# High and low halves of the weight sums stored apart, and the store queue reordered, in the second block of a retention and window-attention trunk

## The reference

```python
def retention_layer(h, w_in, w_out):
    proj = h @ w_in
    q, k, v, g = jnp.split(proj, [D_MODEL, 2 * D_MODEL, 2 * D_MODEL + RET_WIDTH], axis=-1)
    ...                                     # rotary on q and k, decay tables
    sc = jnp.einsum('bnhid,bnhjd->bnhij', qc, kc) * decay_in[None, None]
    o_inner = jnp.einsum('bnhij,bnhje->bnhie', sc, vc)
    ...                                     # scan over chunks: o_cross, state R
    o = o_inner + o_cross
    mu = jnp.mean(o, axis=-1, keepdims=True)
    var = jnp.mean(jnp.square(o - mu), axis=-1, keepdims=True)
    o = ((o - mu) * lax.rsqrt(var + EPS))
    y = o * jax.nn.silu(g)
    return y @ w_out
```

## Time and profile before

| what | value |
|---|---|
| time, median of 3 runs (lowest to highest) | 2474.63 us (2473.95 to 2478.36) |
| profiled execution, its own time | 2476.94 us |
| its span | 2475.1 us |
| PE busy in the span | 2404.5 us, 97% |
| DVE, ACT, POOL busy | 60%, 27%, 18% |
| share of PE in the chain that ended last | 86% (DVE 7%, DMA 4%) |
| DMA traffic | 625.84 MB, mean 253 GB/s |
| heads of block 1, from one load of chunk 0 to the next | 113.2, 115.3 and 112.6 us after the first |

### The profile page before, as it was taken

How to read it: one execution, slowest core, us unless ns; L and a number is a source line. 1 busy time by engine, 2 the same in 40 slices (tenths; PEclk the granted TensorE clock), 3 DMA queues, 4 the chain that set the end, 5 groups by cost and what they waited for, 6 DMA issues and landing times.

```text
span 2475.1 us, 28627 instructions
## 1 busy us (share of the span) xinstructions
PE 2404.5 (97%) x11216; PEld 1972.0 (80%) x11216; DVE 1484.6 (60%) x2037; ACT 679.7 (27%) x1470; POOL 451.1 (18%) x327
## 2 busy tenths in 40 slices
PE   7999999999989999989999999999999999999998
PEld 6888888877867787878888888888888887888886
DVE  6555655677556656663758564655567745557374
ACT  2212312235121212122442231223352312213143
POOL 2111111221245646550001000000001100001000
PEclk9999999999999999999999999999999999999999
DMA  8667565645789798985259878776447987787433
GB/s 351 270 226 289 212 254 226 236 175 217 302 304 394 289 388 302 385 314 200 98 214 318 286 245 290 249 256 217 143 163 233 330 263 278 255 274 252 170 102 145
DMA packets 131833, 625.84 MB, mean 253 GB/s; under 512 B 8864, under 2 KB 9632, under 8 KB 109728
## 3 DMA queue, kind: packets, MB, share of 16 engines
q1 hardware_dynamic: 122864, 588.53, 65.7%
q10 hardware_dynamic: 8880, 36.18, 3.9%
HBM read 471.58 MB, written 153.09 MB: 252 GB/s over the span
## 4 chain that ended last, share of the span: by engine, by line
PE 86%; DVE 7%; DMA 4%; issue 1%; ACT 1%; POOL 1%; SPq 0%; DVEq 0%; POOLq 0%; ACTq 0%
PE ps L691 27%; PE ps L693 27%; PE ps L692 27%; DMA whl<-comb_w 2%; PE ps L1201 2%; DMA vg_w<-ff 1%; DVE ff L2262 1%; PE ps L1211 1%; PE ps L1009 1%; DVE fr L1660 1%; ACT ff L1498 1%; PE ps L839 1%; DVE mx L2302 1%; DVE xlo L1660 0%; DVE ff L2332 0%
## 5 line engine op out<-in xcount | busy, mean ns | idle before, releaser
L691 PE MATMUL ps<-whl,xhi 128*128 128x512 f32 (+1 forms) x1088 | 420.3, 386 | 4.4 <-DVE xlo L1660 2.8
L693 PE MATMUL ps<-whl,xlo 128*128 128x512 f32 (+1 forms) x1088 | 414.0, 380 | 0.0
L692 PE MATMUL ps<-whl,xhi 128*128 128x512 f32 (+1 forms) x1088 | 413.3, 380 | 0.0
L691 PE MATMUL ps<-xhi,whl 128*128 128x512 f32 x768 | 304.0, 396 | 17.6 <-DVE xlo L1664 16.2
L693 PE MATMUL ps<-xhi,whl 128*128 128x512 f32 x768 | 300.4, 391 | 0.0
L692 PE MATMUL ps<-xlo,whl 128*128 128x512 f32 x768 | 299.7, 390 | 0.0
L691 PE MATMUL ps<-whl,fr 128*128 128x512 f32 x640 | 257.9, 403 | 9.8 <-DMA whl<-comb_w 5.7
L693 PE MATMUL ps<-whl,fr 128*128 128x512 f32 x640 | 255.3, 399 | 0.0
L692 PE MATMUL ps<-whl,fr 128*128 128x512 f32 x640 | 254.6, 398 | 0.0
L691 PEld LDWEIGHTS ps<-whl,xhi 128*128 128x128 f32 x1088 | 206.8, 190 | 43.8 <-issue 4.3
L693 PEld LDWEIGHTS ps<-whl,xlo 128*128 128x128 f32 x1088 | 206.5, 190 | 39.4
(11 more groups left out here) (215 smaller groups left out, 3843.7 us busy)
## 6 DMA issues: line engine op xcount, KB each, us to landing
whl<-split_w SPq DMA_DIRECT2D x60, 2048.0 KB, 8.3
whl<-split_w SPq DMA_DIRECT2D x118, 1024.0 KB, 7.0
split_w<-whl SPq DMA_DIRECT2D x44, 2048.0 KB, 7.2
whl<-vg_w SPq DMA_DIRECT2D x64, 1024.0 KB, 6.9
raw<-in_stream SPq DMA_DIRECT2D x44, 1024.0 KB, 9.4
vg_w<-ff SPq DMA_DIRECT2D x32, 1024.0 KB, 7.6
whl<-comb_w SPq DMA_DIRECT2D x32, 1024.0 KB, 7.1
raw<-in_stream SPq DMA_DIRECT2D x50, 512.0 KB, 11.6
```

The lines of the kernel that those rows point to most:

```text
L691: pe.matmul(dst, lhs[0], rhs[0], start=start, stop=False)
L692: pe.matmul(dst, lhs[0], rhs[1], start=False, stop=False)
L693: return pe.matmul(dst, lhs[1], rhs[0], start=False, stop=stop)
```

## The change

The semaphore `comb_stored` becomes two, `comb_hi_stored` and `comb_lo_stored`, and the pair of stores two functions. A high half is stored as soon as POOL has made it, a low half when it is made.

```diff
-                def store_piece(j):
-
-                    sp.wait_ge(comb_lo.sem, at(comb_lo, j + 1))
-                    for i in range(2):
-                        ...
-                        sp.dma_start(dst.rearrange("(q p) n -> p q n", p=P),
-                                     stage[:, i, :].rearrange("p (q n) -> p q n", q=4)).then_inc(comb_stored.sem, 16)
+                def store_part(j, i):
+
+                    made, stored = ((comb_hi, comb_hi_stored), (comb_lo, comb_lo_stored))[i]
+                    sp.wait_ge(made.sem, at(made, j + 1))
+                    ...
+                    sp.dma_start(dst.rearrange("(q p) n -> p q n", p=P),
+                                 stage[:, i, :].rearrange("p (q n) -> p q n", q=4)).then_inc(stored.sem, 16)
```

The waits follow. POOL's high half of piece j waits for the store of the previous high half and for the previous low half to be made; whoever writes a low half waits for the store of the previous low half:

```diff
                 if j > 0:
-                    pool.wait_ge(comb_stored.sem, at(comb_stored, 2 * j))
+                    pool.wait_ge(comb_hi_stored.sem, at(comb_hi_stored, j))
+                    pool.wait_ge(comb_lo.sem, at(comb_lo, j))
...
                 if own_lo:
                     pool.wait_ge(comb_hi.sem, at(comb_hi, j + 1))
+                    pool.wait_ge(comb_lo_stored.sem, at(comb_lo_stored, j))
...
                             dve.wait_ge(comb_hi.sem, at(comb_hi, j + 1))
+                            if j > 0:
+                                dve.wait_ge(comb_lo_stored.sem, at(comb_lo_stored, j))
```

The loads of T1 to T4 wait for both semaphores, and so do the three places that waited for all stores of a head. SP's order changes, and on DVE the two parts of piece 2's low half each move one state update ahead:

```diff
+                store_hi(0)
                 load_split(at, 3, split_rows(h, 3), CHUNK)
-                store_piece(0)
+                store_lo(0)
                 load_piece(h, 2)
+                store_hi(1)
                 load_split(at, 4, split_rows(h, 4), CHUNK)
-                store_piece(1)
+                store_lo(1)
                 load_piece(h, 3)
+                store_hi(2)
                 load_split(at, 5, split_rows(h, 5), CHUNK)
-                store_piece(2)
+                store_lo(2)
                 load_piece(h, 4)
-                store_piece(3)
+                store_hi(3)
                 sp.wait_ge(o_mm.sem, at(o_mm, 4))
...
                     if c == 6:
+                        store_lo(3)
                         load_piece(h, 5)
+                        store_hi(4)
...
-                return lambda: store_piece(4), lambda: store_piece(5)
+
+                def close():
+                    store_hi(5)
+                    store_lo(5)
+
+                return lambda: store_lo(4), close
```

More of the change, by code:

```diff
@@ L303, in build @@
         comb_lo = count("comb_lo", head=PIECES, since=1)
-        comb_stored = count("comb_stored", head=2 * PIECES, unit=16, since=1)
+        comb_hi_stored = count("comb_hi_stored", head=PIECES, unit=16, since=1)
+        comb_lo_stored = count("comb_lo_stored", head=PIECES, unit=16, since=1)
         t_loaded = [count(f"comb_loaded{q}", head=1, unit=16, since=1) for q in range(4)]
@@ L448, in load_comb @@
                 def load_comb(dst, q):
-                    sp.wait_ge(comb_stored.sem, at(comb_stored, 4))
+                    sp.wait_ge(comb_hi_stored.sem, at(comb_hi_stored, 2))
+                    sp.wait_ge(comb_lo_stored.sem, at(comb_lo_stored, 2))
                     sp.dma_start(dst.bitcast(F32), comb_rows(h, q)).then_inc(t_loaded[q].sem, 16)
@@ L466, in load_piece, with store_hi, store_lo @@
                         sp.dma_start(raw[j % 2][:, i * HALF:(i + 1) * HALF].rearrange("p (a n) -> p a n", a=2), src).then_inc(comb_raw[j % 2].sem, 16)
-                def store_piece(j):
-                    sp.wait_ge(comb_lo.sem, at(comb_lo, j + 1))
-                    for i in range(2):
-                        if j < 2:
-                            dst = comb_w[4 * h * P:4 * (h + 1) * P, i, j * 512:(j + 1) * 512]
-                        else:
-                            dst = vg_w[4 * h * P:4 * (h + 1) * P, i, (j - 2) * 512:(j - 1) * 512]
-                        sp.dma_start(dst.rearrange("(q p) n -> p q n", p=P),
-                                     stage[:, i, :].rearrange("p (q n) -> p q n", q=4)).then_inc(comb_stored.sem, 16)
+                def store_part(j, i):
+                    made, stored = ((comb_hi, comb_hi_stored), (comb_lo, comb_lo_stored))[i]
+                    sp.wait_ge(made.sem, at(made, j + 1))
+                    if j < 2:
+                        dst = comb_w[4 * h * P:4 * (h + 1) * P, i, j * 512:(j + 1) * 512]
+                    else:
+                        dst = vg_w[4 * h * P:4 * (h + 1) * P, i, (j - 2) * 512:(j - 1) * 512]
+                    sp.dma_start(dst.rearrange("(q p) n -> p q n", p=P),
+                                 stage[:, i, :].rearrange("p (q n) -> p q n", q=4)).then_inc(stored.sem, 16)
+                def store_hi(j):
+                    store_part(j, 0)
+                def store_lo(j):
+                    store_part(j, 1)
                 if h == 0:
@@ L561, in _ @@
             post_loads(1, last_stores)
-            sp.wait_ge(comb_stored.sem, Place("head", 1, HEADS - 1)(comb_stored, 2 * PIECES))
+            sp.wait_ge(comb_hi_stored.sem, Place("head", 1, HEADS - 1)(comb_hi_stored, PIECES))
+            sp.wait_ge(comb_lo_stored.sem, Place("head", 1, HEADS - 1)(comb_lo_stored, PIECES))
             for b in range(FAST, BLOCKS):
@@ L638, in comb_piece @@
                 if j > 0:
-                    pool.wait_ge(comb_stored.sem, at(comb_stored, 2 * j))
+                    pool.wait_ge(comb_hi_stored.sem, at(comb_hi_stored, j))
+                    pool.wait_ge(comb_lo.sem, at(comb_lo, j))
                 elif at.h > 0:
-                    pool.wait_ge(comb_stored.sem, Place("head", at.b, at.h - 1)(comb_stored, 2 * PIECES))
+                    pool.wait_ge(comb_hi_stored.sem, Place("head", at.b, at.h - 1)(comb_hi_stored, PIECES))
+                    pool.wait_ge(comb_lo_stored.sem, Place("head", at.b, at.h - 1)(comb_lo_stored, PIECES))
                 pool.tensor_scalar(stage[:, 0, :].bitcast(F32R), raw[j % 2], 1.0, 1.0, ALU.mult, ALU.mult).then_inc(comb_hi.sem, 1)
@@ L2043, in one_head @@
                     state_update(0)
+                    if combine:
+                        comb_less_hi(2, (0,))
                     state_lo(1)
@@ L2047, in one_head @@
                     if combine:
-                        comb_less_hi(2, (0,))
+                        comb_less_hi(2, (1,))
                     state_lo(2)
@@ L2051, in one_head @@
                     state_update(2, 2 if last else 1)
-                    if combine:
-                        comb_less_hi(2, (1,))
                     state_lo(3)
@@ L2218, in one_block @@
                 if combine:
-                    dve.wait_ge(comb_stored.sem, Place("head", b, HEADS - 1)(comb_stored, 2 * PIECES))
+                    dve.wait_ge(comb_hi_stored.sem, Place("head", b, HEADS - 1)(comb_hi_stored, PIECES))
+                    dve.wait_ge(comb_lo_stored.sem, Place("head", b, HEADS - 1)(comb_lo_stored, PIECES))
                 spread(rstd, rdiag_done)
```

## The result

| what | before | after |
|---|---|---|
| median of 4 runs each (lowest to highest) | 2476.29 us (2473.95 to 2478.36) | 2460.36 us (2460.11 to 2462.85) |
| ratio after to before, 95% interval | | 0.9938 [0.9921, 0.9955] |
| profiled execution: own time, span | 2476.94, 2475.1 us | 2460.11, 2458.3 us |

The change makes the kernel 16 us faster, where 27 were forecast: the direction is right, the size is not, and 2460.36 lies 0.4 us outside the range.

A forecast was written before the change was run, and what follows sets the result against it. PE, busy 97% of the span, bounds the kernel. Gains of 33.3 us less 3 + 4.3 for S1 give 26.0; with one more, 27 us, so 2447.6 us; range 2439 to 2460.

The forecast's parts named there:

- T2's wait and its tail: PE's wait for the T2 load in block 1's four heads, 5.7 us, and 1.4 us of slow matmuls, both to go.
- the first gap: PE idle before each head's first transposes (L839), 17.8 us, to go entirely, with its 6.8 us tail of slow matmuls.
- DVE's parts of piece 2: Half of piece 2's low half moved ahead of state_lo(1) on DVE, into idle time; price zero.
- rival (b): Slower: DVE's new wait for piece 1's low half, ahead of state_lo(1), delays cross(1); 2476 to 2482 us; chance 0.06.
- rival (c): Stall at L839 stays, its y tile held by the wait for piece 3's low half; 2472 to 2478 us; chance 0.06.
- the price of POOL's wait for the low store: POOL's low half of piece 4 waits for piece 3's low store, delaying S1: 1 us in three heads, 4.3 in the first.
- queue sum: SP's transfers added at 2.7 us per MB (392 GB/s); second head's low store of piece 3 issued 840.6, landed 848.3.
- 5.4 us for the residual stream: First head: two more MB share SP's queue, 5.4 us, about 4.3 of it reaching S1.
- store takes 11 us: Upper end of the S1 loss allowed in each of three heads: 3 us, against the 1 us taken.
- the 4.4 us: Landing time of a 1 MB store by the skill's price; by that alone POOL's new wait costs nothing, 7 us better.
- rival (a): The gap moves down to S1 and T2 in block 1; 13.5 us of gain remain, 2461 us; chance 0.19.
- gaps of 2 us or more ahead of S1 in all heads: Listed sign that the forecast is wrong: PE idle 2 us or more before S1 in every head of block 1.

The follow-up runs named there:

- Experiment 4: Kernel before, with POOL's power (inverse deviation) moved ahead of the high half of piece 3 in block 1; 2469.18 us, ratio 0.9973.
- experiment 3: Changed kernel with POOL's own low half of piece 4 behind the low y sums, and own low halves cut into four instructions; 2437.00 us, ratio 0.9844.
- Experiments 6: Changed kernel with DVE's two parts of piece 2's low half back in their old places; 2472.68 us, ratio 0.9988.
- 9: Kernel of experiment 3 with DVE's two parts of piece 2's low half back in their old places; 2448.35 us, ratio 0.9883.
- experiment 7: Changed kernel with the load of piece 5 issued behind the high store of piece 4, not ahead of it; 2463.59 us, ratio 0.9956.
- experiment 2: Changed kernel with POOL's own low halves cut into four instructions, in their old place; 2460.44 us, ratio 0.9938.
- Experiment 1: Changed kernel with POOL's own low half of piece 4 moved behind the four low parts of the y sums; 2443.62 us, ratio 0.9878.
- experiments 5: Changed kernel with SP's old order, stores back in pairs, split semaphores kept; 2458.61 us, ratio 0.9932.
- 8: Kernel of experiment 3 with SP's old order, stores back in pairs, split semaphores kept; 2460.04 us, ratio 0.9930.

## Why the prediction was wrong, step by step

| term | forecast, us | read from the rows, us |
|---|---|---|
| idle at the first transposes, slow matmuls behind, the transposes | 26.2 | 26.2 |
| T2's wait and its tail | 7.1 | 7.1 |
| idle at S1 and at the last transposes | -6.3 | -10.8 |
| slow matmuls behind S1 | 0 | -4.6 |
| the end of the block | 0 | -4.3 |
| sum | 27.0 | 13.6 |

The span fell by 2475.1 - 2458.3 = 16.8 us, so 3.2 us of gain stand in no row that I can name. PE's idle time fell by 10.2 us (70.6 to 60.4), of which the rows explain 9.8; the open part lies almost all in the time in which PE is at work. The right column is a reading and not a closed account.

**Right: the first gap.** No head has an idle time before its first transposes. On POOL the high half of piece 3 is done well before the variances, and the power starts 0.1 us behind them (timelines of DVE and POOL, second head; the earlier trace rows have 4.7 us between the two):

```profile
825.65 0.23 DVE L2088 TENSOR_SCALAR ov<-mv,rcol 128x4 f32<-128x4 f32 x1 [0.15 <-DVE mv L2065]
```
```profile
825.97 1.02 POOL L631 TENSOR_TENSOR ors<-ov,mhalf 128x4 f32<-128x4 f32 x1 [6.97 <-DVE ov L2088]
```

Experiment 4 confirms the cause by itself, as far as it goes (three heads of four).

**Right: T2.** Nothing is left of the 5.7 us of the earlier trace rows. A late S1 also gives T2 more time; in experiment 3, where S1 is not late, 2.6 us of the wait come back, in the first head alone.

**Right that it costs nothing, but its worth was not priced: DVE's parts of piece 2.** PE waited nowhere for DVE's new wait, which came to 1.43 us in the first head and to nothing in the others. In the second head the part ends at 808.47 and the low part of the state follows at 808.74, after 0.27 us of waiting for ACT (timeline of DVE, second head):

```profile
807.25 1.22 DVE L1987 TENSOR_TENSOR ff<-raw,ff 128x1024 fp32r<-128x1024 f32 x1
808.74 1.28 DVE L1686 SCALAR_TENSOR_TENSOR fr<-state,rcol,fr 128x1024 fp32r<-128x1024 f32 x1 [0.27 <-ACT fr L1502]
```

That answers rival (b), and with the first gap rival (c) falls too. But "price zero" names only the cost. Experiments 6 and 9 show what the move is good for, 12 and 11 us: it keeps POOL's early high half off the low part of the state, and it sends the low store of piece 2 off 8 us sooner. The second of these was in the forecast's working without a price: the low half made at 823.7 is the second part in its new place; in its old one it would end at 828.33 + 1.22 = 829.55.

**Wrong: the price of POOL's wait for the low store.** This is the step that failed: "I allow 1 us loss in each of three heads", plus 4.3 in the first. The forecast put S1 4.9 us after the end of the gate tiles. PE frees chunk 5 at the end of those tiles, and SP then issues T2, at 841.26; S1 starts at 848.79, 7.5 us later, 2.6 more than forecast. The store accounts for that. By the forecast's queue sum (issued at 840.6, landed at 848.3) it was to take 7.7 us, and it took 10.5 (10.3 to 10.5 in three heads; 13.9 in the first, where the forecast's 5.4 us for the residual stream make 13.1). SP's timeline, second head:

```profile
823.98 0.81 SPq L453 DMA_DIRECT2D fr<-comb_w  x2
829.44 0.53 SPq L453 DMA_DIRECT2D whl<-comb_w  x1
830.02 0.61 SPq L522 DMA_DIRECT2D whl<-split_w  x1
831.81 0.38 SPq L478 DMA_DIRECT2D vg_w<-ff  x1
```

Ahead of it stand 4 MB issued within 8 us, and the DMA engines are full, but at 359 GB/s, not at the 392 of the earlier trace rows that I had used:

```profile
824.00:842.00 18.00, 18.00 (x87) 14.90 (x86) 10.35 (x13) 6.74 (x11) 10.53 (x6) 1.00 1.00 359
```

By the queue sum of the forecast, 5 MB from 824.0 end at 837.5 at 2.7 us each and at 838.6 at 2.92 each, with 2.1 us more at 840.7: that explains 8.9 of the 10.5 us. The last 1.6 us stay open; experiment 7 refutes one cause, what is issued behind. So of the 2.8 us too few 1.1 are the rate and the rest is open. That the median of all stores in the earlier trace rows is 7.7 as well is an accident, and I took it for support, although the same change had put this store behind 4 MB of loads. Over block 1 the stores of the changed kernel land at

```profile
DMA to landing us min/median/max: 5.1/10.5/15.1
```

against 4.2/7.7/15.9 in the earlier trace rows. The 3 us for "store takes 11 us" that the forecast named as its worst case was nearly the ordinary case, and I had taken 1. By the 4.4 us that the forecast worked out from the Trainium skill (SBUF — State Buffer, the DMA setup-cost knee) no wait would have come; no store of block 1 landed that soon in the changed kernel, and it is no price for a store behind a full queue.

**Left out: the slow matmuls.** Each of these waits, 2.8 to 6.5 us, has a tail, as the forecast itself had said of the first gap. At S1 it put the tail at nothing, without a reason. I count about 32 matmuls at 0.43 us behind S1 in four heads against 9 before, 23 x 0.20 = 4.6 us.

**Left out: the port.** I weighed the rule of the Trainium skill on GpSimd and VectorE at one short DVE part, where it came to nothing. It bore on two other places, both beside the own low half, the longest of POOL's instructions in the block. One is the last gate product, 4.95 and 4.73 us in place of 0.69 in the third and fourth head. The forecast had booked 1 us of gain here, on the guess that the two would no longer run side by side. In the first two heads the product starts ahead of POOL and is not held. In the other two DVE took PE's wait over from POOL; experiment 2 shows that it added nothing to it. The other is the end of the block, where the kernel makes rounded copies for the next step. DVE's timelines of the changed kernel and of the kernel before:

```profile
1088.15 3.69 DVE L2229 CAST vwin<-vwin 64x256 fp32r<-64x256 f32 x1
```
```profile
1109.59 0.29 DVE L2205 CAST vwin<-vwin 64x256 fp32r<-64x256 f32 x1
```

POOL's subtraction ran from 1087.14 for 4.55 us, so the copy ended 0.15 us behind it. The rule as cited is on operations with two inputs, and the copy has one; that it was held by the same port is my reading. PE waited 3.75 us for what DVE makes next, 0.82 before, with about 15 half-width matmuls at the lower clock behind it: 2.9 + 1.4 = 4.3 us. In experiment 2, with the four short instructions, this wait is 1.6. In experiments 1 and 3 it is 1.0 and 0.4, but there the copy runs ahead of that subtraction.

**The rivals.** The time is that of rival (a), 2461, but only half of its mechanism came true, and the match of the number is luck. Its 13.5 us do not follow from its terms: less 9 for S1, three tails of 2.2 and the 7.1 of T2, 27 leaves 4.3 us, 2470. S1 is late as it said, with the slow matmuls behind; T2 is not late, and what (a) had for T2 was taken by the end of the block. I had given (a) 0.19 and cut the range in its middle. Of the signs of being wrong, "gaps of 2 us or more ahead of S1 in all heads" came true, in two heads at S1 and in two at the transposes just ahead of it. The DMA share of 0.89 in the earlier trace rows spoke for it: it rose to 0.96 in the second head, 0.01 above what the rival reckoned with.

**One error behind these.** I had priced the wait on POOL by what the store is late, and never asked why S1's sums stand behind it. The store and S1 have nothing to do with one another; only POOL's program order ties them, as it had tied the power to the store. Nor is this tie new. In the kernel before POOL's high half of piece 4 waited for the stores of piece 3, with the own low half and the y sums behind it (timeline of POOL, second head):

```profile
852.56 1.90 POOL L642 TENSOR_SCALAR ff<-raw 128x2048 fp32r<-128x2048 f32 x1 [4.11 <-DMA vg_w<-ff]
```

That wait was hidden, since the gate tiles came later too. The change removed the tie at the power, left this one, and put the low store that it hangs on behind T4, T3 and T1. Experiment 1 removes it.

## What to carry to other kernels

When a buffer's wait is loosened on an in-order engine, look for the waits that the change leaves or adds in the same queue and for what stands behind them: a short operation that the critical engine needs belongs ahead of every operation that waits for DRAM. Price a store by the bytes issued ahead of it, at the lowest rate seen in a full stretch and not the highest, do not take the median of all stores for support, and add the slow matmuls behind each wait of TensorE. Do not judge one part of such a change by taking it alone: SP's order was worth 0 us beside the own low half in the old place and 23 us with it moved (experiments 5 and 8 against the changed kernel and experiment 3).

## What the runs showed of the hardware

- One long GpSimd subtraction (128 x 2048, 4.54 us) stretched a VectorE product that started 0.14 us behind it from 0.69 to 4.95 us, and another, 4.55 us, a copy of 64 x 256 from 0.29 to 3.69. With the subtraction cut into four of 128 x 512 a product that started 0.31 us behind the first took 1.52 and the copy 1.08; the four took 5.07 us together, 7.00 beside busier VectorE work. A GpSimd operation with one input, 1.90 us, did the same to a VectorE one with two: 2.87 in place of 1.28. This agrees, the copy apart, with the rule of the Trainium skill named above, and in these rows the harm is the size of the instruction on GpSimd.
- With reads and writes mixed the DMA engines were full (share 1.00) at 359 GB/s over 18 us; another full stretch, of the kernel before, moved 392.
- A store of 1 MB behind 4 MB of loads landed 10.3 to 10.5 us after its issue in three heads, and the load issued directly behind it had no part in that (11.3 us without it, in the second head).
